# Four of a layer's eleven down-projection units computed as seven block products, with VectorE forming the sums

## What is computed

```python
    for i in range(DEPTH):
        ...
        h = rms_norm(x, ffn_norm[i])
        u = causal_depthwise_conv(h @ w_up[i], conv_w[i], conv_b[i])
        x = x + (jax.nn.silu(u[..., :D_FF]) * u[..., D_FF:]) @ w_down[i]
        x = x + (p[i] @ ple_proj[i]) * jax.nn.sigmoid(x @ ple_gate[i])
```

## Time and profile before

| | us |
|---|---|
| median of 3 runs | 662.86 (662.07 to 662.92) |
| span of the profiled execution | 661.4 |
| TensorE busy | 653.2 |
| VectorE busy | 441.5 |
| ScalarE busy | 420.2 |
| GpSimd busy | 402.8 |

### The profile page before, as it was taken

One profiled execution on the slowest core, in us unless ns is written; L12 is line 12 of the kernel. 1 busy time (PEld: TensorE's weight loads), 2 busy tenths in 40 slices (PEclk: granted clock), 3 DMA queues, 4 the chain that ended last, 5 costly groups with the idle time before them and its releaser, 6 DMA issues.

```text
span 661.4 us, 9574 instructions
## 1 busy us (share of the span) xinstructions
PE 653.2 (99%) x3792; PEld 562.9 (85%) x3792; DVE 441.5 (67%) x637; ACT 420.2 (64%) x633; POOL 402.8 (61%) x212
## 2 busy tenths in 40 slices
PE   8999999999999999999999999999999999999997
PEld 6988887888888888888889879878888888888885
DVE  5997778758989985003488777875798989810033
ACT  6669886677767675334474879756777777733332
POOL 5443510288888887987841353005888888889871
PEclk9999999999999999999999999999999999999999
DMA  9972125675565555553387421165555555555411
GB/s 318 363 257 64 66 105 158 201 236 191 191 190 192 192 191 190 191 191 107 108 283 248 156 100 64 65 207 176 192 190 191 191 192 191 191 191 190 160 33 63
DMA packets 74606, 115.37 MB, mean 174 GB/s; under 512 B 2369, under 2 KB 58433, under 8 KB 74305
## 3 DMA queue, kind: packets, MB, share of 16 engines
q1 hardware_dynamic: 73408, 111.95, 50.8%
q10 hardware_dynamic: 1152, 2.81, 1.2%
HBM read 113.70 MB, written 1.05 MB: 174 GB/s over the span
## 4 chain that ended last, share of the span: by engine, by line
PE 95%; DVE 2%; DMA 1%; ACT 0%; issue 0%; SPq 0%; ACTq 0%
PE ps L1516 24%; PE ps L963 15%; PE ps L964 14%; PE ps L965 14%; PE ps L1518 12%; PE ps L1109 1%; PE ps L1015 1%; DMA raw<-w_in 1%; PE ps L1135 1%; PE ps L1375 1%; PE ps L977 1%; PE ps L1050 1%; PE ps L1147 1%; DVE hn L2110 1%; PE ps L1539 1%; PE ps L1541 1%
## 5 line engine op out<-in xcount | busy, mean ns | idle before, releaser
L461 POOL TENSOR_TENSOR wl<-raw,wh 128x2048 fp32r<-128x2048 f32 (+1 forms) x74 | 332.6, 4499 | 86.3 <-ACT wh L590 86.3
L1516 PE MATMUL ps<-hT_hl,wh 128*128 128x512 f32 x688 | 238.6, 392 | 0.0
L590 ACT ACTIVATE wh<-raw 128x2048 fp32r<-128x2048 f32 (+1 forms) x100 | 180.6, 1809 | 77.0 <-PE ps L965 69.4
L1518 PE MATMUL ps<-hT_hl,wl 128*128 128x256 f32 x688 | 193.3, 281 | 0.0
L1516 PEld LDWEIGHTS ps<-hT_hl,wh 128*128 128x128 f32 x688 | 129.1, 188 | 28.2
L1518 PEld LDWEIGHTS ps<-hT_hl,wl 128*128 128x128 f32 x688 | 129.4, 188 | 0.0
L963 PE MATMUL ps<-wh,hT_hl 128*128 128x512 f32 (+1 forms) x216 | 79.7, 369 | 0.0
L965 PE MATMUL ps<-wh,hT_hl 128*128 128x512 f32 (+1 forms) x216 | 77.4, 359 | 0.0
L964 PE MATMUL ps<-wl,hT_hl 128*128 128x512 f32 (+1 forms) x216 | 77.3, 358 | 0.0
L2041 DVE TENSOR_TENSOR x<-x,ps 128x512 f32<-128x512 f32 x16 | 10.8, 686 | 99.1 <-PE ps L965 98.7
L448 POOL TENSOR_SCALAR st<-st 128x2 f32<-128x2 f32 (+3 forms) x22 | 6.5, 295 | 114.6 <-ACT lat L665 62.2
(11 more groups left out here) (321 smaller groups left out, 1182.9 us busy)
## 6 DMA issues: line engine op xcount, KB each, us to landing
raw<-w_up SPq DMA_DIRECT2D x44, 1024.0 KB, 5.1
raw<-w_down SPq DMA_DIRECT2D x22, 1024.0 KB, 4.9
raw<-w_in SPq DMA_DIRECT2D x16, 1024.0 KB, 9.9
raw<-w_o SPq DMA_DIRECT2D x6, 1024.0 KB, 5.1
raw<-ple_gate SPq DMA_DIRECT2D x6, 1024.0 KB, 4.9
raw<-w_in SPq DMA_DIRECT2D x4, 704.0 KB, 5.6
ng<-norm_gains ACTq DMA_DIRECT2D x2, 1024.0 KB, 6.6
raw<-w_o SPq DMA_DIRECT2D x4, 512.0 KB, 3.9
```

The source lines that it names most:

```text
L461: pool.tensor_tensor(wl[:, slot, 0:n], raw[:, slot, 0:n], w_high(u)[:, 0:n].bitcast(F32), ALU.subtract).then_inc(done, 1)
L590: act.activation(w_high(u)[:, c:n], raw[:, slot, c:n], ACT.Copy).then_inc(h_made, 1)
L1516: pe.matmul(both, high[:, c], hU_all[:, k].rearrange("p a n -> p (a n)"), start=k == 0, stop=False, skip_group_check=True)
L1518: mm = pe.matmul(o, wl[:, slot, c], hU_h[:, k, :], start=False, stop=k == KT - 1, skip_group_check=True)
```

## The change

In down units 3, 5, 7 and 9 (`SEVEN`) the 256 x 256 activations and the 256 x 1024 weights are taken as 2 x 2 blocks (128 x 128 and 128 x 512), and the product is formed by the Strassen-Winograd scheme from seven block products in place of eight. Each is still three matmuls of 512 columns, so the unit has 21 in place of 24 (`down_seven`).

VectorE forms the four sums of weights in 128 x 512 blocks (`weight_sums`, one of them in place in `raw`) and the four sums of activations in 128 x 128 blocks (`act_sums`). ScalarE rounds both (`seven_high`), and VectorE subtracts for their low parts (`act_rest`, `weight_rest`). The low part `wl` of down units 3 to 10 moves from GpSimd to VectorE (`down_low`); GpSimd keeps those of down units 0 to 2 and of the gate.

The products go to banks 1 to 7 in place of 0 to 3 alone: three of the seven products are in banks 1, 2, 3 where they belong to one output quarter only, and four gather in banks 4 to 7 over all four units. After the last such unit ScalarE copies banks 6 and 5 to `both_sums` and `minus_both` (rows of `qk_swa`), and VectorE combines them into `x` with eight instructions, ahead of `add_to_x`.

```diff
+SEVEN = (3, 5, 7, 9)
+FEW = len(SEVEN)
+DVE_FROM = 3
+def eights(s):
+    return s - sum(f < s for f in SEVEN)
...
+        def quarter_sums(i):
+            return hT_hl[:, (i % 2) * 1536:(i % 2 + 1) * 1536]
+        def quarter_highs(i):
+            return (proj_h, pt_r)[i % 2][:, 0:1536]
...
-                for u in range(U_POOL, UNITS):
+                for u in (*range(U_POOL, U_DOWN + DVE_FROM), *range(U_GATE, UNITS)):
                     low(u)
...
+                def seven_high(i):
+                    u = U_DOWN + SEVEN[i]
+                    if i > 1:
+                        unit_done(act, layer, U_DOWN + SEVEN[i - 2])
+                    act.wait_ge(F["a_sums"], base["a_sums"] + i + 1)
+                    act.activation(a_high[:, i % 2, 0:3 * P], g_flat(SEVEN[i], True)[:, P:4 * P],
+                                   ACT.Copy)
+                    act.activation(a_high[:, i % 2, 3 * P:7 * P], g_flat(SEVEN[i], False), ACT.Copy
+                                   ).then_inc(F["a_rounded"], 1)
+                    if i == 1:
+                        act.wait_ge(F["prod"], base["prod"] + STEPS - 1)
+                        act.wait_ge(F["g_low"], base["g_low"] + eights(STEPS - 1))
+                    act.wait_ge(F["w_sums"], base["w_sums"] + 4 * i + 4)
+                    act.activation(quarter_highs(i), quarters[:, i % 2], ACT.Copy
+                                   ).then_inc(F["w_rounded"], 1)
...
-                for u in range(U_DOWN + 3, U_GATE + 1):
-                    high(u)
-
-
-
+                for s in range(DVE_FROM, STEPS):
+                    if s in SEVEN:
+                        act.wait_ge(F["w_sums"], base["w_sums"] + 4 * SEVEN.index(s) + 2)
+                    high(U_DOWN + s)
+                    if s in SEVEN:
+                        seven_high(SEVEN.index(s))
+                high(U_GATE)
+                act.wait_ge(F["sevens_done"], base["sevens_done"] + 1)
+                for o, bank in ((both_sums, 6), (minus_both, 5)):
+                    act.activation(o, ps[:, bank, :], ACT.Copy).then_inc(F["sevens_copied"], 1)
                 high(U_GATE + 1)
...
+                def down_seven(i):
+                    s = SEVEN[i]
+                    slot, high = unit(U_DOWN + s)
+                    raw_a, sums_a = (g(s).rearrange("p k n -> p (k n)") for g in (g_high, g_low))
+                    rounded = a_high[:, i % 2]
+                    a = [(rounded[:, n * P:(n + 1) * P],
+                          raw_a[:, (n + 1) * P:(n + 2) * P] if n < 3 else
+                          sums_a[:, (n - 3) * P:(n - 2) * P]) for n in range(7)]
+                    a11, a22, a12, s1, s2, s3, s4 = a
+                    def product(bank, act, b_h, b_l, n):
+                        c = slice(n * 512, (n + 1) * 512)
+                        own = bank >= 4
+                        return split_product(ps[:, bank, :], *act, b_h[:, c], b_l[:, c],
+                                             own and i == 0, own and i == FEW - 1)
+                    pe.wait_ge(F["a_rest"], base["a_rest"] + i + 1)
+                    if i == 0:
+                        pe.wait_ge(F["conv_done"], base["conv_done"] + 4 * STEPS)
+                    low = wl[:, slot]
+                    product(4, a11, high, low, 1)
+                    product(3, a12, high, low, 3)
+                    product(2, s4, high, low, 2)
+                    product(5, s1, high, low, 0)
+                    pe.wait_ge(F["w_rest"], base["w_rest"] + i + 1)
+                    high, low = quarter_highs(i), quarter_sums(i)
+                    product(6, s2, high, low, 0)
+                    mm = product(7, s3, high, low, 1)
+                    if i == FEW - 1:
+                        mm.then_inc(F["sevens_done"], 1)
+                    product(1, a22, high, low, 2).then_inc(w_used, 1)
                 for s in range(STEPS):
-                    pe.wait_ge(F["g_low"], base["g_low"] + s + 1)
+                    if s in SEVEN:
+                        down_seven(SEVEN.index(s))
+                        continue
+                    pe.wait_ge(F["g_low"], base["g_low"] + eights(s + 1))
...
+                    o = g_flat(s, True).rearrange("p (k n) -> p k n", k=2) if s in SEVEN else g
+                    tt(o, g, cv[s % 2][:, 2:4, :], ALU.mult).then_inc(F["prod"], 1)
...
+                def weight_sums(i):
+                    u = U_DOWN + SEVEN[i]
+                    slot = u % DEEP
+                    dve.wait_ge(raw_landed[slot],
+                                (layer * (UNITS // DEEP) + u // DEEP + 1) * 16)
+                    unit_done(dve, layer, U_DOWN + SEVEN[i - 2] if i > 1 else U_DOWN - 1)
+                    b12, b11, b22, b21 = (raw[:, slot, n * 512:(n + 1) * 512] for n in range(4))
+                    t2, t3, t4 = (quarters[:, i % 2, n * 512:(n + 1) * 512]
+                                  for n in range(3))
+                    tt(t3, b12, b22, ALU.add).then_inc(F["w_sums"], 1)
+                    for n, (o, one, two) in enumerate(((b12, b12, b11), (t2, b12, b22),
+                                                       (t4, t2, b21))):
+                        tt(o, one, two, ALU.add).then_inc(F["w_sums"], 1)
+                        if n < 2:
+                            dve.wait_ge(F["w_sums"], base["w_sums"] + 4 * i + n + 2)
+                def act_sums(i):
+                    dve.wait_ge(F["prod"], base["prod"] + SEVEN[i] + 1)
+                    a21, a11, a22, a12 = (g_flat(SEVEN[i], True)[:, n * P:(n + 1) * P]
+                                          for n in range(4))
+                    s1, s2, s3, s4 = (g_flat(SEVEN[i], False)[:, n * P:(n + 1) * P]
+                                      for n in range(4))
+                    chained(tt(s1, a21, a22, ALU.subtract))
+                    tt(s3, a11, a21, ALU.subtract)
+                    chained(tt(s2, s1, a11, ALU.subtract))
+                    tt(s4, a12, s2, ALU.add).then_inc(F["a_sums"], 1)
+                def act_rest(i):
+                    dve.wait_ge(F["a_rounded"], base["a_rounded"] + i + 1)
+                    rounded = a_high[:, i % 2].bitcast(F32)
+                    s = SEVEN[i]
+                    raw_a, sums_a = (g(s).rearrange("p k n -> p (k n)") for g in (g_high, g_low))
+                    tt(raw_a[:, P:4 * P], g_flat(s, True)[:, P:4 * P], rounded[:, 0:3 * P],
+                       ALU.subtract)
+                    tt(sums_a, g_flat(s, False), rounded[:, 3 * P:7 * P], ALU.subtract
+                       ).then_inc(F["a_rest"], 1)
+                def weight_rest(i):
+                    dve.wait_ge(F["w_rounded"], base["w_rounded"] + i + 1)
+                    o = quarter_sums(i)
+                    tt(o, quarters[:, i % 2], quarter_highs(i).bitcast(F32), ALU.subtract
+                       ).then_inc(F["w_rest"], 1)
+                def down_low(s):
+                    u = U_DOWN + s
+                    slot = u % DEEP
+                    dve.wait_ge(h_made, highs(layer, u))
+                    tt(wl[:, slot], raw[:, slot], w_high(u).bitcast(F32), ALU.subtract
+                       ).then_inc(F["down_low"], 1)
+                for s in range(DVE_FROM, STEPS):
+                    if s + 1 in SEVEN and s > DVE_FROM:
+                        weight_sums(SEVEN.index(s + 1))
+                        act_sums(SEVEN.index(s + 1))
+                    elif s in SEVEN and s == DVE_FROM:
+                        weight_sums(0)
+                        act_sums(0)
+                    down_low(s)
+                    if s in SEVEN:
+                        act_rest(SEVEN.index(s))
+                        weight_rest(SEVEN.index(s))
+                dve.wait_ge(F["sevens_copied"], base["sevens_copied"] + 2)
+                parts = [x[:, t, c] for t, c in map(quarter, range(4))]
+                chained(tt(both_sums, both_sums, ps[:, 4, :], ALU.add))
+                chained(tt(minus_both, minus_both, both_sums, ALU.subtract))
+                tt(parts[2], parts[2], minus_both, ALU.add)
+                chained(tt(both_sums, both_sums, ps[:, 7, :], ALU.add))
+                chained(tt(parts[1], parts[1], both_sums, ALU.add))
+                chained(tt(minus_both, minus_both, ps[:, 7, :], ALU.subtract))
+                tt(parts[0], parts[0], minus_both, ALU.add)
+                chained(tt(parts[3], parts[3], ps[:, 4, :], ALU.add))
                 add_to_x("down_done", U_GATE - 1, "x_mlp")
```

More of the change, by code:

```diff
@@ L141 @@
     "wo_done": 3, "x_mid": 4, "low_copied": 2 * STEPS, "halves_summed": 2 * STEPS, "tap2": 4 * STEPS, "tap1": 4 * STEPS, "conv_done": 4 * STEPS,
-    "silu": STEPS, "prod": STEPS, "g_high": STEPS, "g_low": STEPS,
+    "silu": STEPS, "prod": STEPS, "g_high": STEPS - FEW, "g_low": STEPS - FEW,
+    "w_sums": 4 * FEW, "a_sums": FEW, "a_rounded": FEW, "a_rest": FEW, "w_rounded": FEW, "w_rest": FEW,
+    "down_low": STEPS - DVE_FROM, "sevens_done": 1, "sevens_copied": 2,
```

(29 more changed lines are left out.)

5 lines of the change are left out of this document (2 added, 3 removed).

## The result

The changed kernel takes 683.15 us (median of 4 runs, 682.30 to 683.57) against 662.86: a ratio of 1.0311, 95% interval 1.0299 to 1.0324. The forecast was 683.7.

The account below looks back on a forecast made before the run. TensorE was taken to bound the kernel, busy 653.2 of 661.4 us. Two layers of 1.6 (down stage) + 6.8 (tail) + 2.0 (clock) add 20.8 to 662.86, giving 683.7 us; own range 680 to 687, wider range 669 to 688.

Parts of the forecast that it names:

- VectorE's list: Down stage: a seven-product unit costs VectorE 8.7 us, a pair of units 10.9, where TensorE needs 10.2.
- The waits of the stage: Layer 0 down stage: TensorE waits 4.3 us before units 3, 4, 6, 8, against 2.7 saved; ends 1.6 later.
- The tail: Down stage's end to gate: GpSimd's gate low parts hold up the combining instructions, adding 6.8 us a layer.
- The question that I had left open: Tail: whether GpSimd's second gate low part or the third combining instruction goes first; moves the end by half a microsecond.
- The clock: Behind TensorE's 6.4 us idle before the gate, the clock falls to 1.2 GHz: 2.0 us a layer, bounds 0 and 2.7.
- The rival without a drop: Same forecast, but the clock stays up behind the idle time: 679.7 us; chance 0.17.
- The sum: Whole kernel: 2 x (1.6 + 6.8 + 2.0) = +20.8 us, giving 683.7 by the median.
- GpSimd doesn't hold the combining instructions: Rival, tail: additions end 4.9 us earlier and TensorE keeps its clock; +3.5 us a layer, 669.9; chance 0.14.
- VectorE keeps up: Rival, down stage: VectorE's SBUF work runs at 0.8 of the rows' lengths with GpSimd silent; 658.2 us; chance 0.06.
- Worse than the forecast: Rival: the 2.8 us stall also drops the clock, or VectorE's lists contend with ScalarE's and DMA writes; 688 to 696; chance 0.06.

Follow-up runs that it names:

- the kernel without GpSimd's wait: Against the kernel with seven-product units 4, 6, 8 and repaired order (658.38 us): GpSimd's gate low parts no longer wait for the combination; 668.37 us.
- the kernel kept at work: Against the changed kernel: 24 idle 512-column matmuls on TensorE between down unit 10 and the transposes of x; 679.75 us, ratio 1.0262.

## Why the prediction was right

**VectorE's list.** 8.7 us for a seven-product unit was forecast, 8.66 measured; the straight line between row lengths gave 1.67 for 1536 columns, where the next instruction starts 1.67 later in the trace. A pair of units was to take VectorE 10.9 us, and takes 10.86. The low part of unit 4 was forecast for 272.7; TensorE started on it at 272.52.

**The waits of the stage.** The forecast was 0.1 + 2.8 + 0.7 + 0.7 = 4.3 us. The waits that the view gives in layer 0 are 2.62 + 0.40 + 0.41, which less the 2.72 us saved would leave only 0.7, where the stage is 1.6 us longer. By the starts of the matmuls the sum holds: unit 4 starts at 272.52, 2.9 us later than 93 matmuls in a row behind the first at 248.55; units 6 and 8 lose 0.65 each, and the restart of unit 8 another 0.1; 4.3 in all. So these terms were right, layer 1 apart, where the clock took the place of the last two. The experiments confirm the causes: without the sums no wait, with the other order no wait of 2.6 us.

**The tail.** Forecast: second combining instruction ends 307.4, third 312.3, combination 315.8, last addition 318.3. Measured: 307.20, 312.18, 315.55, 318.07. The question that I had left open, who goes first when GpSimd and the third instruction both want SBUF, fell as assumed here: GpSimd began at 307.04, the third instruction at 307.24. In the kernel without GpSimd's wait GpSimd began first both times as well; with the low part ahead of the next sums VectorE was first, and GpSimd was the one delayed.
The Trainium skill (SBUF — State Buffer, Who interferes with whom) states that a VectorE instruction with two SBUF inputs contends with a GpSimd instruction that reads SBUF, and one with at most one SBUF input doesn't. The rows here agree: 4.94, 4.39 and 4.25 us against 0.67 to 0.69 for the instructions that read PSUM.

**The clock.** This is the term that was mis-sized: 2.0 us a layer forecast, 1.1 by the rows of the kernel kept at work, 1.2 by its span and 1.7 by its median. That it falls was right: granted clock 0.66 and 0.67 behind the stage. The rival without a drop, 679.7, is refuted, and comes out (679.75) when TensorE is kept at work. I had taken the start of the program for the pattern, where work of 4.5 us ran slow; here 3.3 us of the slow stretch passed while TensorE was idle (the window from 313.00 to 316.30), and it was over with the transposes.
The Trainium skill (TensorE: Matmul & The Clock Gate, What's actually happening) says that the throttled state is the default and that activity releases it. The trace agrees: the clock fell while TensorE was idle, and the gate matmuls behind the transposes run at full speed again.

**The sum.** The span grew by 680.5 - 661.4 = 19.1 us, of 20.8 forecast; the median by 20.3. The 1.2 us between them lie in which executions were profiled. Every run's time on record is 1.69 to 1.85 us above its own span, not 1.5. The profiled execution of the changed kernel is the fastest of its four (682.30 us, 0.85 below the median); that of the kernel before, with 661.4 + 1.75, would be an estimated 663.1 us, 0.3 above its median. So the nearness of the forecast to the median is luck in part: by the profiled pair it is 1.7 us too long, which is the clock term, 0.8 us a layer; by the medians 0.5.

**The rivals.** "GpSimd doesn't hold the combining instructions" fails on the 4.94 us. "VectorE keeps up" fails on 0.69 us an addition with GpSimd idle throughout. "Worse than the forecast" had a condition that came true: the stall ahead of unit 4 dropped the clock in layer 1. It cost nothing, since the waits ahead of units 6 and 8 fell away for it. The gain that the scheme offers is real, and the kernel with three such units has it.

## What to carry to other kernels

Where TensorE is full, work taken from it pays only if the engine that gets the exchange work keeps its deadlines: write its list with lengths from the trace and compare it unit by unit, not as a share of busy time (VectorE was at 67%). Place the last such unit early enough that the combination lies under what remains. A VectorE instruction with both inputs in SBUF that meets a GpSimd low part ends behind it, so one of 0.69 us took up to 4.94 here; a wait added on GpSimd was worth 10.0 us of 668. And read what a wait costs from the starts of TensorE's matmuls: a wait given as 0.40 us cost 0.65.

## What I had not expected of the hardware

TensorE's clock fell behind an idle stretch of 1.93 us in the kernel with GpSimd's second gate low part held (granted clock 0.52 in the stretch after it). In the changed kernel it fell behind one of 2.59 us in layer 1 (starts 0.43 us apart), but not behind the 2.62 us in layer 0 of the same program. A stretch of a couple of microseconds can thus cost the clock or not, in one and the same run.

Where TensorE had to wait for VectorE anyway, a fallen clock cost nothing: the two down stages of the changed kernel are 61.42 and 61.40 us long, one at full clock, the other with 3 us at half. It is a near thing: the clock took 1.5 us where the waits had taken 1.4. In the kernel without the combination the clock fell in layer 0 and eight matmuls ran slow at 0.43 us a start, in place of five in the changed kernel; there the part of the stage from unit 4 on took 37.51 us, against 37.24.
